# Attention scores as split products, with x parked in DRAM

## The chip, the cores and the metric

The kernel runs on one core of one Trainium2 chip, in one launch. The time is the device time of the whole program in microseconds (us), the median of a few executions. Engines are called TensorE (PE), VectorE (DVE), ScalarE (ACT), GpSimd (POOL) and SyncE (SP).

## The reference, cut to what matters

Two decoder layers on a sequence of 256 tokens with 2048 features, all in float32. Layer 0 has a convolution and DeltaNet mixer, layer 1 sparse attention; behind each mixer and behind each SwiGLU block stands a residual and a layer norm. The change lies in layer 1:

```
q, k_c, v_c, k_s, v_s, k_w, v_w, gates = split(x @ w_in)      # 16 query heads, 4 groups, head dim 128
q, k_s, k_w = rope(q), rope(k_s), rope(k_w)
k_cmp, v_cmp = compress(k_c), compress(v_c)                   # 15 compressed blocks per group
sc = einsum('bghsd,bgnd->bghsn', q, k_cmp) * 128 ** -0.5      # compressed branch
sc = einsum('bghqd,...', q, k_s or k_w)    * 128 ** -0.5      # selected and window branch
p = softmax(where(valid, sc, -1e30))                          # each branch
o = gate0 * p_c @ v_cmp + gate1 * p_s @ v_s + gate2 * p_w @ v_w
x = layer_norm(alpha * x + o @ w_out)
```

With 256 tokens all 4 blocks of 64 are selected and the window of 512 covers everything, so both the selected and the window branch are plain causal attention over 256 keys, each with keys and values of its own.

## The kernel before

Every dense product is done in three passes of split operands: a float32 array `w` is kept as `w_hi` (rounded to the fp32r format by a ScalarE copy, L708) and `w_lo` (the rest, a VectorE subtraction, L1253). `passes` (L2041) then issues hi x hi, hi x lo and lo x hi. Weights come in slabs of 1 MB, on SP's queue, into 4 `raw` slots, and are split by halves of a slab into 4 slots of `w_hi` and `w_lo`. `halves(n)` on ScalarE and on VectorE stands for the next n halves; ScalarE's waits until TensorE has used the half four before (`half_used`), VectorE's for ScalarE's, and TensorE's for VectorE's (`w_lo_ready`). The order of all work on each engine is written out by hand.

In layer 1 the four groups `g` of 4 query heads are worked through one after the other, with two tiles `t` of 128 tokens. For each, TensorE does:

- `scores(g, t)`: one PSUM bank `("c", g, t)` for the 4 heads against 15 compressed keys (L2595), and for each branch `b` `t + 1` banks `("s", g, t, b, k)` against `kn` = 128 (t + 1) keys (L2604). These are float32 matmuls of `qT` with `kcmpT` and `ksT`; each of them stands in the trace as two loads and two multiplies.
- `compressed_T`, `branch_T`: the scaled probabilities are turned.
- `outputs(g, t)`: the split probabilities times the split values, into `("ao", g, t)`.
- `queries(g + 1)`: the next group's turned queries, after VectorE's `rope`.
- `fill(n)`: n halves (12 passes each, two token tiles) of the query projection's next chunk, and behind its last, of the output projection `out1` (`out_halves`). For that product the attention output must be split too: `early_split(kt)` on both engines.

These use PSUM banks 4 to 7 in turn: use number `K[name]` must wait until use `K[name] - 4` has been read (`sp_free`).

VectorE in `scores(g, t)` (L1897) drains each bank with scale and mask (L1904, L1914) and takes the maximum of each branch (L1906, L1918), each of which releases ScalarE's `exps` of that branch (L1136). `scaled` multiplies by gate over sum (L1938, L1941). `put_T` (L1868) copies turned keys and queries out of PSUM (L1872). `compressed_lo`, `branch_lo` (L1956, L1964) and ScalarE's `compressed_hi`, `branch_hi` (L1149, L1157) split the turned probabilities. `rope_stage` (L1100) on ScalarE takes a chunk out of its banks for VectorE's `rope` (L1854 to L1866), `heads_out` (L1159) takes `ao` to `qT`.

The residual `x` stays in SBUF from the last norm on until `first_moments(2)` (L1374) adds it.

Of the kernel before, what the change touches and what calls it, by code (L numbers as in the profile page):

```python
# [13 lines left out]
F32 = mybir.dt.float32  # L14
# [7 lines left out]
P = 128  # L22
# [59 lines left out]
def trunk(nc, x_in, positions, ln_mix_g, ln_mix_b, ln_ffn_g, ln_ffn_b, ffn_w_in, ffn_w_out,  # L82
          hy_w_in, sc_conv_w, dn_conv_w, dn_a_log, dn_dt_bias, dn_norm_w, hy_w_out,
          nsa_w_in, cmp_pos_k, cmp_w1_k, cmp_w2_k, cmp_pos_v, cmp_w1_v, cmp_w2_v, nsa_w_out,
          inv_freq, ln_by_feature, end_positions, x_by_feature, gc_rows, beta_rows, out, stop=None):
# [3 lines left out]
    with ctx:  # L89
# [121 lines left out]
        kcmpT = part(64)  # L211
        assert used == 10944
# [20 lines left out]
        sc_buf = [[base[:, 1024 * n:1024 * n + 1024] for n in range(2)] for base in (gb_flat, sc_more)]  # L233
# [5 lines left out]
        v_cmp = sb("v_cmp", [P, NG * DH], F32R, offset=big_at + 4 * 10944)  # L239
        p_far = sb("p_far", [P, 2, 2, 512], F32R, offset=gb_at + 4 * 2048)  # L240
        p_near = [sb(f"p_near{n}", [P, 512], F32R, offset=gb_at + 4 * (512 + 1024 * n)) for n in range(2)]
# [5 lines left out]
        v_hi_ready, v_lo_ready = sem("v_hi_ready"), sem("v_lo_ready")  # L247

# [93 lines left out]
        def scores_use(g, t):  # L342
            uses([("c", g, t)] + [("s", g, t, b, k) for b in range(2) for k in range(t + 1)])
# [226 lines left out]
        def _(pool):  # L570
# [116 lines left out]
        def _(act):  # L687
# [401 lines left out]

            def put_hT(name):  # L1090
# [27 lines left out]
            halves(5)  # L1118
            name = ("vcmp",)
# [5 lines left out]
            halves(8)  # L1125
            keep_values(1, C["kv"] + 1)

            def exps(g, t, parts):
# [3 lines left out]
                for n in parts:  # L1132
                    act.wait_ge(for_act, FA[("scores", g, t, n)])
                    v = sc_buf[t][n - 1][:, 0:HPG * kn].rearrange("p (h n) -> p h n", h=HPG) if n else sc_cmp[t]
# [33 lines left out]
            values_hi(0)  # L1168
            exps(0, 0, range(3))
            halves(1)  # L1170
            for g in range(NG):
                exps(g, 1, (0, 1))
                halves(1)
                compressed_hi(g, 0)
# [23 lines left out]
                if g < NG - 1:  # L1198
                    exps(g + 1, 0, range(3))
# [15 lines left out]
        def _(dv):  # L1215
# [158 lines left out]
            def first_moments(n):  # L1374
# [3 lines left out]
                else:  # L1378
                    dv.wait_ge(x_in_sem, 16 * NT)
                for c in range(4):  # L1380
# [487 lines left out]
            def put_T(k, dst):  # L1868

                for a in range(2):  # L1870
                    dv.wait_ge(sp_ready[(k + a) % 4], (k + a) // 4 + 1)
                    dv.tensor_copy(dst(a), bank[4 + (k + a) % 4][:, :].rearrange("p (h t) -> p h t", h=2)).then_inc(sp_free[(k + a) % 4], 1)  # L1872
            for b in range(2):
# [6 lines left out]
                if b == 0:  # L1880
                    name = ("kcmpT",)
                    wait_sp(dv, name)
                    sp_out(dv.tensor_copy(kcmpT[:, 0:NCG], sp_bank(name)[:, 0:NCG]), name)
                else:
                    put_T(K[("kv", 0, 0)], lambda a: ksT[:, 0, 2 * a:2 * a + 2, :])
                rope(C["kv"] if b else C["kvk"])
            halves(8)
            put_T(K[("kv", 1, 0)], lambda a: ksT[:, 1, 2 * a:2 * a + 2, :])
# [8 lines left out]
            def scores(g, t):  # L1897
# [5 lines left out]
                v = sp_bank(name)[:, 0:HPG * NCMP].rearrange("p (h n) -> p h n", h=HPG)  # L1903
                sp_out(dv.scalar_tensor_tensor(sc_cmp[t], v, SCALE, bc(neg_cmp[:, t, :], HPG), ALU.mult, ALU.add), name)  # L1904
                wait_sp_read(dv, name)
                to_act(dv.tensor_reduce(nmax[:, 0:4], sc_cmp[t], AX.X, ALU.max, negate=True))  # L1906
                for b in range(2):
                    v = sc_buf[t][b][:, 0:HPG * kn].rearrange("p (h n) -> p h n", h=HPG)
                    hp = HPG // (t + 1)
# [821 lines left out]
```

## Time and profile before

| | us |
|---|---|
| median of 3 runs | 2351.47 (2351.12 to 2352.3) |
| the profiled execution | 2353.08, its span 2351.4 |
| TensorE multiply, loads | 2324.8, 1962.4 busy |
| VectorE, ScalarE, GpSimd | 1575.1, 1132.9, 34.3 busy |
| granted TensorE clock, mean | 0.998 |

All times in the trace are in us from the start of the span. A multiply's end is modelled, since matmuls are pipelined: what one costs is the distance to the next one's start. A row's bracket says how long the engine was idle ahead of it, and what released it.

### The profile page before, as it was taken

The page shows a single profiled execution, that of the slowest core. Times are in us where ns is not written, and L with a number is a line of the kernel's source. Part 1 is how long each engine was busy: PE and PEld are TensorE (multiplying, and loading weights), DVE is VectorE, ACT ScalarE, POOL GpSimd, SP SyncE. Part 2 cuts the span into 40 slices and gives each one's busy share as a digit, 9 for nine tenths or more (in the row PEclk, how much of TensorE's full clock was granted, in tenths as well). Part 3 has the DMA queues.
Part 4 walks back from the last instruction along what each step waited for, and adds up shares of the span by engine and source line. Part 5 has one row for each costly group of instructions (what it writes and reads, how often), then busy time and mean ns, then how long its engine had stood idle before and what let it go on. Part 6 is the DMA issues. An engine that isn't in the chain of part 4 may idle for free.

```text
span 2351.4 us, 30551 instructions
## 1 busy us (share of the span) xinstructions
PE 2324.8 (99%) x11559; PEld 1962.4 (83%) x11559; DVE 1575.1 (67%) x2075; ACT 1132.9 (48%) x1560; POOL 34.3 (1%) x79
## 2 busy tenths in 40 slices
PE   9999999999999999999999999999999999999998
PEld 8899988888888888888888887778888888888886
DVE  6767785676666666755578758867766666665556
ACT  5446654554434444444465546656444344444443
POOL 1000000100000000000000000000000000000001
PEclk9999999999999999999999999999999999999999
DMA  7555442745555555655546653254655565565553
GB/s 271 188 188 194 163 146 91 298 138 196 193 196 196 191 188 195 231 197 193 188 173 226 226 179 97 101 197 163 206 190 193 196 196 183 196 228 197 196 193 111
DMA packets 180486, 440.03 MB, mean 187 GB/s; under 512 B 7352, under 2 KB 19776, under 8 KB 166064
## 3 DMA queue, kind: packets, MB, share of 16 engines
q1 hardware_dynamic: 177456, 424.70, 53.8%
q0 software_dynamic: 2368, 13.13, 1.5%
q8 instruction: 54, 0.88, 0.2%
q10 hardware_dynamic: 576, 1.05, 0.1%
q14 instruction: 32, 0.26, 0.0%
HBM read 436.74 MB, written 2.11 MB: 187 GB/s over the span
## 4 chain that ended last, share of the span: by engine, by line
PE 88%; DVE 7%; ACT 4%; issue 1%; DMA 1%; SPq 0%; DVEq 0%; ACTq 0%
PE bank L2043 26%; PE bank L2045 26%; PE bank L2044 26%; PE bank L2056 4%; PE bank L2057 2%; DVE w_lo L1253 2%; PE bank L2381 1%; ACT w_hi L708 1%; DMA raw<-in_hy_w_in_dram 1%; ACT yt L783 1%; ACT sc_more L1136 1%; ACT gb L1136 1%; PE bank L2353 0%; DVE sm L1918 0%; ACT xt_both L794 0%
## 5 line engine op out<-in xcount | busy, mean ns | idle before, releaser
L1253 DVE TENSOR_TENSOR w_lo<-raw,w_hi 128x1024 fp32r<-128x1024 f32 x765 | 929.5, 1224 | 664.3 <-ACT w_hi L708 660.8
L708 ACT ACTIVATE w_hi<-raw 128x1024 fp32r<-128x1024 f32 x765 | 805.8, 1060 | 1007.8 <-PE bank L2045 922.2
L2043 PE MATMUL bank<-w_hi,xt_both 128*128 128x512 f32 x1888 | 740.9, 392 | 6.1 <-DVE w_lo L1253 2.8
L2045 PE MATMUL bank<-w_hi,xt_both 128*128 128x512 f32 x1888 | 735.9, 390 | 0.0
L2044 PE MATMUL bank<-w_lo,xt_both 128*128 128x512 f32 x1888 | 735.7, 390 | 0.0
L2043 PEld LDWEIGHTS bank<-w_hi,xt_both 128*128 128x128 f32 x1888 | 354.9, 188 | 80.8 <-issue 6.3
L2045 PEld LDWEIGHTS bank<-w_hi,xt_both 128*128 128x128 f32 x1888 | 354.8, 188 | 74.3
L2044 PEld LDWEIGHTS bank<-w_lo,xt_both 128*128 128x128 f32 x1888 | 354.9, 188 | 72.2
L2045 PE MATMUL bank<-w_hi,a_lo 128*128 128x512 f32 x664 | 258.4, 389 | 0.0
L2043 PE MATMUL bank<-w_hi,a_hi 128*128 128x512 f32 x664 | 258.4, 389 | 0.0
L2044 PE MATMUL bank<-w_lo,a_hi 128*128 128x512 f32 x664 | 258.4, 389 | 0.0
L2056 PE MATMUL bank<-xt_both,w_hi 128*128 128x512 f32 x488 | 172.8, 399 | 1.9 <-DVE xt_both L1510 1.3
L1468 DVE STREAM_TRANSPOSE big<-yt 32x256 f32<-32x256 f32 x352 | 153.5, 436 | 10.0
L2043 PEld LDWEIGHTS bank<-w_hi,a_hi 128*128 128x128 f32 x664 | 124.6, 188 | 26.1
L2045 PEld LDWEIGHTS bank<-w_hi,a_lo 128*128 128x128 f32 x664 | 124.6, 188 | 25.9
L2044 PEld LDWEIGHTS bank<-w_lo,a_hi 128*128 128x128 f32 x664 | 124.6, 188 | 25.7
L2057 PE MATMUL bank<-xt_both,w_lo 128*128 128x256 f32 x488 | 137.2, 281 | 0.0
L2043 PE MATMUL bank<-xt_both,w_hi 128*128 128x256 f32 x400 | 116.8, 292 | 0.3 <-DVE w_lo L1253 0.3
L2045 PE MATMUL bank<-xt_both,w_lo 128*128 128x256 f32 x400 | 113.2, 283 | 0.0
L2044 PE MATMUL bank<-xt_both,w_hi 128*128 128x256 f32 x400 | 113.2, 283 | 0.0
L2056 PEld LDWEIGHTS bank<-xt_both,w_hi 128*128 128x128 f32 x488 | 91.8, 188 | 25.2 <-DVE xt_both L1510 1.6
L2057 PEld LDWEIGHTS bank<-xt_both,w_lo 128*128 128x128 f32 x488 | 92.2, 189 | 0.0
(343 smaller groups left out, 1794.0 us busy)
## 6 DMA issues: line engine op xcount, KB each, us to landing
raw<-in_ffn_w_in_dram SPq DMA_DIRECT2D x176, 1024.0 KB, 5.0
raw<-in_ffn_w_out_dram SPq DMA_DIRECT2D x88, 1024.0 KB, 4.9
raw<-in_hy_w_in_dram SPq DMA_DIRECT2D x53, 1024.0 KB, 5.1
raw<-in_nsa_w_in_dram SPq DMA_DIRECT2D x41, 1024.0 KB, 5.1
raw<-in_hy_w_out_dram SPq DMA_DIRECT2D x16, 1024.0 KB, 5.0
raw<-in_nsa_w_out_dram SPq DMA_DIRECT2D x16, 1024.0 KB, 5.1
raw<-in_cmp_w_k_dram SPq DMA_DIRECT2D x4, 1024.0 KB, 6.8
raw<-in_cmp_w_v_dram SPq DMA_DIRECT2D x4, 1024.0 KB, 6.4
```

Source lines behind the costliest of these rows:

```text
L708: act.activation(weights_of(h)[0], half_of(h), ACT.Copy).then_inc(w_hi_ready, 1)
L783: ins = act.activation(yt[:, kt, tok], src[:, a * P:(a + 1) * P], ACT.Identity, bias=lnT[:, 1, kt:kt + 1], scale=lnT[:, 0, kt:kt + 1])
L1136: ins = act.activation(v[:, h, :], v[:, h, :], ACT.Exp, bias=nmax[:, 4 * n + h:4 * n + h + 1], accum_out=sums[:, 4 * n + h:4 * n + h + 1])
L1253: dv.tensor_tensor(lo, src, hi.bitcast(F32), ALU.subtract).then_inc(w_lo_ready, 1)
L1468: ins = dv.transpose(dst, src)
L2043: pe.matmul(dst, l_hi, r_hi, start=start, stop=False, skip_group_check=shared)
L2044: pe.matmul(dst, l_hi, r_lo, start=False, stop=False, skip_group_check=shared)
L2045: return pe.matmul(dst, l_lo, r_hi, start=False, stop=stop, skip_group_check=shared)
L2056: pe.matmul(b[f][:, :], hi[:, v], xt_both[:, kt, :, :], start=kt == 0, stop=False, skip_group_check=True)
L2057: ins = pe.matmul(b[f][:, 0:SEQ], lo[:, v], xt_hi[:, kt, :], start=False, stop=kt == KT - 1, skip_group_check=True)
L2381: ins = pe.matmul(b[:, h * P:(h + 1) * P], lhs(h), rhs(h), start=True, stop=True)
```

## The change

- The turned keys go, split, to `k_split`, in place of `x`: `[hi/lo, group, branch, token]`, so that the two branches' keys of a group lie side by side. The turned queries of one group go to `q_split`. ScalarE copies the high part out of PSUM (`keys_hi`, `queries_hi`), VectorE subtracts (`turned_lo_out`, in place of `put_T`). The compressed keys are split by VectorE alone, with 16 columns a group.
- `scores` issues three passes for each head: 16 columns for the compressed keys, `2 * kn` for both branches at once. A bank `("s", g, t, k)` now holds both branches of 2 heads (t = 0) or of 1 head (t = 1). VectorE drains all banks of a tile, and then takes the two maxima.
- `x` is stored to DRAM on POOL's queue after the loads of `w2`, and loaded again after `("ao", 3, 0)`; ScalarE waits for the store ahead of `keys_hi(0)`, VectorE for the load in `first_moments(2)`.
- In TensorE's loop `fill(1), outputs(g, 0), fill(1)` becomes `fill(2), outputs(g, 0)`. On ScalarE `rope_stage` comes before `heads_out` and `compressed_hi`, and in group 3 the early splits before `compressed_hi(3, 0)`. In group 2 the splits 2 and 3 come before VectorE's `rope` and ScalarE's `branch_hi(2, 1)`.
- The buffers of scores and probabilities are laid out anew (`sc_both`, `probs`, `p_near`).

```
@@ POOL, ahead of layer_norm(2)
+                for t in range(NT):
+                    pool.dma_start(x_rows[t * P:(t + 1) * P, :], x[:, t, :]).then_inc(x_out, 16)
+                pool.wait_ge(x_out, 16 * NT)
+                wait_sp(pool, ("ao", NG - 1, 0))
+                for t in range(NT):
+                    pool.dma_start(x[:, t, :], x_rows[t * P:(t + 1) * P, :]).then_inc(x_back, 16)
@@ ScalarE
+            def queries_hi(g):
+                for a in range(2):
+                    name = ("q", 2 * g + a)
+                    wait_sp(act, name)
+                    act.activation(q_split[:, 0, 2 * a:2 * a + 2, :], sp_bank(name)[:, :].rearrange("p (h t) -> p h t", h=2), ACT.Copy)\
+                       .then_inc(t_hi_ready, 1)
...
             halves(5)
+            act.wait_ge(x_out, 16 * NT)
+            keys_hi(0)
             name = ("vcmp",)
             wait_sp(act, name)
...
             for g in range(NG):
                 exps(g, 1, (0, 1))
                 halves(1)
+                if g == NG - 1:
+                    for kt in range(8, EARLY["out1"]):
+                        early_split("out1", kt)
                 compressed_hi(g, 0)
                 for b in range(2):
                     branch_hi(g, 0, b)
                 exps(g, 1, (2,))
                 halves(3)
-                heads_out(g, 0)
-                if g == NG - 1:
-                    for kt in range(8, EARLY["out1"]):
-                        early_split("out1", kt)
                 if g == NG - 2:
                     for kt in range(2):
                         early_split("out1", kt)
-                compressed_hi(g, 1)
                 if g < NG - 1:
                     rope_stage(C["q"] + g + 1, FA[("rope", g)])
-                for b in range(2):
-                    branch_hi(g, 1, b)
+                heads_out(g, 0)
+                compressed_hi(g, 1)
                 if g == NG - 2:
                     for kt in range(2, 4):
                         early_split("out1", kt)
+                for b in range(2):
+                    branch_hi(g, 1, b)
...
                 halves(2)
                 if g < NG - 1:
+                    queries_hi(g + 1)
                     exps(g + 1, 0, range(3))
@@ VectorE
-            def put_T(k, dst):
+            def turned_lo_out(name, n, hi, lo):
+                dv.wait_ge(t_hi_ready, n)
+                dv.tensor_tensor(lo, sp_bank(name)[:, :].rearrange("p (h t) -> p h t", h=2), hi.bitcast(F32), ALU.subtract)\
+                  .then_inc(sp_free[K[name] % 4], 1)
...
-                    sp_out(dv.tensor_copy(kcmpT[:, 0:NCG], sp_bank(name)[:, 0:NCG]), name)
+                    own(dv.tensor_scalar(kcmp_split[:, :, :].rearrange("p a n -> p (a n)"), ones[:, :], 0.0, None, ALU.mult))
...
+                    own(dv.tensor_copy(hi, src))
+                    sp_out(dv.tensor_tensor(lo, src, hi.bitcast(F32), ALU.subtract), name)
... in scores(g, t)
+                for k in range(2 * (t + 1)):
+                    name = ("s", g, t, k)
+                    wait_sp(dv, name)
+                    ins = dv.scalar_tensor_tensor(both[:, 2 * hp * k:2 * hp * (k + 1), :], sp_bank(name)[:, :].rearrange("p (m n) -> p m n", n=kn),
+                                                  SCALE, bc(mask, 2 * hp), ALU.mult, ALU.add)
+                    sp_out(ins, name)
+                for k in range(2 * (t + 1)):
+                    wait_sp_read(dv, ("s", g, t, k))
                 for b in range(2):
+                    v = probs(t, b)
                     to_act(dv.tensor_reduce(nmax[:, 4 + 4 * b:8 + 4 * b], v, AX.X, ALU.max, negate=True))
@@ TensorE
                 for h in range(HPG):
-                    ins = pe.matmul(b[:, h * NCMP:(h + 1) * NCMP], qT[:, 4 * g + h, v], kcmpT[:, g * NCMP:(g + 1) * NCMP], start=True, stop=True)
+                    ins = passes(b[:, 16 * h:16 * h + 16], q_split[:, 0, h, v], q_split[:, 1, h, v], *kc, True, True)
...
+                for k in range(2 * (t + 1)):
+                    name = ("s", g, t, k)
+                    b = sp_use(name)
+                    for j in range(hp):
+                        h = hp * k + j
+                        ins = passes(b[:, j * 2 * kn:(j + 1) * 2 * kn], q_split[:, 0, h, v], q_split[:, 1, h, v], *keys, True, True)
+                    sp_done(ins, name)
...
-                fill(1)
+                fill(2)
                 outputs(g, 0)
-                fill(1)
                 compressed_T(g, 1)
```

## Rows read from the trace of the kernel before

**Rows 1.** The page's busy times of the engines, shares of the span.
```profile
PE 2324.8 (99%) x11559; PEld 1962.4 (83%) x11559; DVE 1575.1 (67%) x2075; ACT 1132.9 (48%) x1560; POOL 34.3 (1%) x79
```

**Rows 2.** Waits, 1395 to 1560 us: who for whom, total, times, longest.
```profile
PEld bank L2625 <- DVE p_cmp L1956: 2.5, 4, 0.9
PE bank L2043 <- ACT yt L1104: 1.7, 1, 1.7
...
PE bank L2043 <- DVE p_far L1964: 1.3, 4, 0.3
PE bank L2043 <- DVE xt_both L1291: 1.2, 1, 1.2
```

**Rows 3.** Timeline of TensorE, score blocks: start, length, line, shapes, count.
```profile
1440.32 0.96 PE L2595 MATMUL bank<-big 128*128 128x15 f32 x8
1441.13 2.03 PE L2604 MATMUL bank<-big 128*128 128x128 f32 x16
1442.92 0.48 PE L2043 MATMUL bank<-w_hi,xt_both 128*128 128x512 f32 x1
...
1530.54 3.70 PE L2604 MATMUL bank<-big 128*128 128x256 f32 x16
1533.89 0.58 PE L2043 MATMUL bank<-w_hi,xt_both 128*128 128x512 f32 x1
```

**Rows 4.** Timeline of TensorE, split products of 512 and 256 columns.
```profile
1229.04 0.39 PE L2056 MATMUL bank<-xt_both,w_hi 128*128 128x512 f32 x1
1229.26 0.28 PE L2057 MATMUL bank<-xt_both,w_lo 128*128 128x256 f32 x1
1229.38 0.40 PE L2056 MATMUL bank<-xt_both,w_hi 128*128 128x512 f32 x1
```

**Rows 5.** Timeline of group 0, second tile, 1412 to 1428 us.
```profile
1412.72 1.28 DVE L1914 SCALAR_TENSOR_TENSOR sc_more<-bank,big 128x512 f32<-128x512 f32 x2
...
1415.35 0.51 ACT L1136 ACTIVATE sc_more<-sc_more,sm 128x256 f32<-128x256 f32 x1 [1.25 <-DVE sm L1918]
...
1418.42 1.23 DVE L1253 TENSOR_TENSOR w_lo<-raw,w_hi 128x1024 fp32r<-128x1024 f32 x1 [0.58 <-ACT w_hi L708]
...
1425.49 3.49 DVE L1253 TENSOR_TENSOR w_lo<-raw,w_hi 128x1024 fp32r<-128x1024 f32 x3
...
1427.24 0.48 PE L2043 MATMUL bank<-w_hi,xt_both 128*128 128x512 f32 x1
```

**Rows 6.** Timeline of group 1, first tile, 1442 to 1448 us.
```profile
1442.31 0.69 DVE L1914 SCALAR_TENSOR_TENSOR gb<-bank,big 128x512 f32<-128x512 f32 x1 [0.52 <-PE bank L2604]
...
1443.75 0.40 ACT L1136 ACTIVATE gb<-gb,sm 128x128 f32<-128x128 f32 x1 [0.66 <-DVE sm L1918]
...
1447.05 0.23 DVE L1929 RECIPROCAL sm<-sm 128x12 f32<-128x12 f32 x1 [1.88 <-ACT gb L1136]
```

**Rows 7.** Timeline of group 3, 1545 to 1550 us.
```profile
1545.88 1.33 ACT L727 ACTIVATE xt_both<-big 128x256 fp32r<-128x256 f32 x4
...
1546.32 1.43 DVE L1291 TENSOR_TENSOR xt_both<-big,xt_both 128x256 fp32r<-128x256 f32 x4 [0.60 <-ACT xt_both L727]
...
1549.04 0.47 PE L2043 MATMUL bank<-w_hi,xt_both 128*128 128x512 f32 x1 [1.42 <-DVE w_lo L1253]
```

**Rows 8.** Timeline of the turned keys, 1344 to 1352 us.
```profile
1344.61 1.17 ACT L1122 ACTIVATE v_cmp<-bank 15x512 fp32r<-15x512 f32 x2
...
1346.00 0.68 DVE L1878 TENSOR_TENSOR v_cmp<-bank,v_cmp 15x512 fp32r<-15x512 f32 x1
1346.71 1.29 DVE L1872 COPY big<-bank 128x512 f32<-128x512 f32 x2
...
1351.85 0.85 PEld L2570 LDWEIGHTS bank<-ident,yt 128*128 128x128 f32 x8 [0.57 <-DVE yt L1866]
```

**Rows 9.** DMA issues (KB each, us to landing) and POOL's timeline.
```profile
x<-in_x_dram POOLq DMA_DIRECT2D x2, 1024.0 KB, 10.0
...
1242.12 0.72 POOL L661 DMA_DIRECT2D big<-in_cmp_w_k_dram  x1 [274.80 <-DVE x L1414]
```

More of the change, by code:

```diff
@@ L210, in trunk @@
         cmp_hT = part(128, "p (k n) -> p k n", k=2)
-        kcmpT = part(64)
-        assert used == 10944
+        kcmp_at = big_at + 4 * used
+        used += 128
+        assert used == 11008
         used += NG * DH
@@ L232, in trunk, with probs @@
         sc_more = sb("sc_more", [P, 2048], offset=a_at)
-        sc_buf = [[base[:, 1024 * n:1024 * n + 1024] for n in range(2)] for base in (gb_flat, sc_more)]
+        sc_both = [gb_flat[:, 0:1024], sc_more[:, 0:2048]]
+        def probs(t, b):
+            return sc_both[t].rearrange("p (h b n) -> p h b n", h=HPG, b=2)[:, :, b, :]
         kc_flat = kcT.rearrange("p b h t -> p (b h t)")
@@ L247, in trunk @@
         v_hi_ready, v_lo_ready = sem("v_hi_ready"), sem("v_lo_ready")
+        t_hi_ready, x_out, x_back = sem("t_hi_ready"), sem("x_out"), sem("x_back")
         def unit_no(g, t, b, k=0):
@@ L342, in scores_use @@
         def scores_use(g, t):
-            uses([("c", g, t)] + [("s", g, t, b, k) for b in range(2) for k in range(t + 1)])
+            uses([("c", g, t)] + [("s", g, t, k) for k in range(2 * (t + 1))])
         def probs_use(g, t):
@@ L1088, in _, with keys_hi @@
                .then_inc(sp_free[K[("gates",)] % 4], 1)
+            def keys_hi(b):
+                for a in range(2):
+                    name = ("kv", b, a)
+                    wait_sp(act, name)
+                    act.activation(k_split[:, 0, 2 * a:2 * a + 2, b, :], sp_bank(name)[:, :].rearrange("p (h t) -> p h t", h=2), ACT.Copy)\
+                       .then_inc(t_hi_ready, 1)
+            def queries_hi(g):
+                for a in range(2):
+                    name = ("q", 2 * g + a)
+                    wait_sp(act, name)
+                    act.activation(q_split[:, 0, 2 * a:2 * a + 2, :], sp_bank(name)[:, :].rearrange("p (h t) -> p h t", h=2), ACT.Copy)\
+                       .then_inc(t_hi_ready, 1)
             def put_hT(name):
@@ L1125, in _ @@
             halves(8)
+            keys_hi(1)
             keep_values(1, C["kv"] + 1)
@@ L1168, in _ @@
             values_hi(0)
+            queries_hi(0)
             exps(0, 0, range(3))
@@ L1379, in first_moments @@
                     dv.wait_ge(x_in_sem, 16 * NT)
+                if n == 2:
+                    dv.wait_ge(x_back, 16 * NT)
                 for c in range(4):
@@ L1969, in turned_q @@
             def turned_q(g):
-                put_T(K[("q", 2 * g)], lambda a: qT[:, 4 * g + 2 * a:4 * g + 2 * a + 2, :])
+                for a in range(2):
+                    hi, lo = (q_split[:, n, 2 * a:2 * a + 2, :] for n in range(2))
+                    turned_lo_out(("q", 2 * g + a), 4 + 2 * g + a + 1, hi, lo)
             halves(3)
@@ L1993, in _ @@
                 compressed_lo(g, 1)
+                if g == NG - 2:
+                    for kt in range(2, 4):
+                        early_split("out1", kt)
                 if g < NG - 1:
@@ L2593, in scores @@
                 b = sp_use(name)
+                kc = [kcmp_split[:, n, 16 * g:16 * g + 16] for n in range(2)]
                 for h in range(HPG):
-                    ins = pe.matmul(b[:, h * NCMP:(h + 1) * NCMP], qT[:, 4 * g + h, v], kcmpT[:, g * NCMP:(g + 1) * NCMP], start=True, stop=True)
+                    ins = passes(b[:, 16 * h:16 * h + 16], q_split[:, 0, h, v], q_split[:, 1, h, v], *kc, True, True)
                 sp_done(ins, name)
                 kn = (t + 1) * P
-                hp = HPG // (t + 1)
-                for br in range(2):
-                    for k in range(t + 1):
-                        name = ("s", g, t, br, k)
-                        b = sp_use(name)
-                        for h in range(hp):
-                            ins = pe.matmul(b[:, h * kn:(h + 1) * kn], qT[:, 4 * g + hp * k + h, v], ksT[:, br, g, 0:kn], start=True, stop=True)
-                        sp_done(ins, name)
+                hp = 2 // (t + 1)
+                keys = [k_split[:, n, g, :, 0:kn] for n in range(2)]
+                for k in range(2 * (t + 1)):
[5 more added lines that the diff above has]
+                    sp_done(ins, name)
             def compressed_T(g, t):
```

45 lines of the change are left out of this document (21 added, 24 removed).

## The prediction, before the change was run

> **What bounds the kernel now.** I read the page's busy table first, then the waits of the attention stage, then the three engines' instructions in order of time. The table says that TensorE works through the whole span [rows 1]: a change pays only if it takes TensorE work away, or takes away one of the few places where TensorE waits. The waits [rows 2] name those places, about 9 us in all where the four heads' groups are worked through (1402 to 1562 us): in each group's `outputs(g, 0)`, which waits for VectorE's low parts (the 2.5 and 1.3 us), in group 2 for ScalarE's `rope_stage` and for an early split, and in group 3 for a low half of weights [rows 7]. Everywhere else there a fill (a half slab of the next dense product, 12 passes) follows without a gap. Behind the attention stage TensorE again works without gaps, so what is late or early at its end is late or early at the end of the span, one for one.
>
> **The score products themselves.** Today one compressed block of scores takes 1440.32 to 1441.13 = 0.81 us, a `t == 0` block 1441.13 to 1442.92 = 1.79 us, a `t == 1` block 1530.54 to 1533.89 = 3.35 us [rows 3]. A float32 matmul stands in the trace as two load-and-multiply records (4 heads give x8), 0.10 to 0.11 us each when it has few columns. The split form has 3 records of 4 heads = 12 in each block: 512 columns cost 0.22 to 0.23 us a record, 256 columns 0.12 [rows 3, 4]. So `t == 1` falls to 12 x 0.227 = 2.72 (-0.63), `t == 0` to 12 x 0.12 = 1.44 (-0.35). For 16 moving columns the trace has no split product. Nearest are the float32 records with 15 columns: 12 x 0.112 = 1.35 (+0.5). If the load of 128 stationary columns were hidden, it could be as little as 0.3 in all; the upper bound is a doubled record, 2.7. I take 1.35, since 15 and 128 columns cost nearly the same today (0.10 and 0.11) [rows 3], so it is the load that is paid. Per group: -0.63 - 0.35 + 2 x 0.5 = 0.0. The products save TensorE nothing.
>
> The Trainium skill (TensorE: Matmul & The Clock Gate, "Back-to-back issue gap") puts a matmul of 1 to 64 columns at a floor of about 25 ns, and its section "LDWEIGHTS (loading the stationary operand)" a load at columns / 1.2, 107 ns for 128. By the first alone the compressed block would cost 0.3 us; by the second 1.28. The rows side with the second.
>
> **The order of VectorE and ScalarE.** This is where I expect the time to go. A bank now holds both branches of the same heads. Before, VectorE drained branch 0 (2 steps), reduced it to its maximum, and ScalarE began its exponentials while VectorE did branch 1. Now all four banks are drained before the first maximum. In group 0, `t == 1`: two drains from 1412.72 take 1.28, ScalarE's exponentials start 1415.35, its next weight half lies behind them, and VectorE's low half waits 0.58 for that, until 1418.42 [rows 5]. Two more drains lie before the first maximum: +1.22 (two of 0.62, less one wait). ScalarE has no gap from 1415.35 on that could take this up: exponentials, half, `compressed_hi`, `branch_hi`, exponentials of branch 1, and then VectorE's scaling and its next low halves, the first done at about 1426.7 [rows 5] (three from 1425.49 in 3.49). TensorE needs that half at 1427.24: slack 0.55.
>
> For `t == 0` the same: a first drain at 1442.31, exponentials from 1443.75, and VectorE sits idle 1.88 until they end [rows 6]; now compressed block +0.5 and one more drain before the maximum, less 0.2 for the shorter bank: about +0.87 on the exponentials, hence on the next halves and on the start of `scores(g, 1)`. It adds to the first. So the first half behind `scaled(g, 1)` comes 0.87 + 1.22 = 2.1 us later, minus the slack 0.55: **+1.5 us in group 0 and +1.5 in group 1**, although the fill put ahead of `outputs(g, 0)` (one fill, 12 x 0.227 = 2.7 us, against (2.5 + 1.3) / 4 = 0.95 us of waits there) does hide the low parts; the wait moves to the halves behind it.
>
> Group 2. The waits for `rope_stage` (1.7) and for the early split (1.2) [rows 2]. The first is bounded anew: ScalarE now stages rope before `heads_out` and `compressed_hi`, but its exponentials end 2.1 us later, and by my count it ends where it did: 0. The second goes, since VectorE splits 2 and 3 before rope: -1.4 with its restart. **-1.4 in group 2.** What is late next there is VectorE, which reaches `scores(3, 0)` some 0.5 us behind TensorE: +0.4 into group 3.
>
> Group 3. ScalarE's four early splits (1.33 us from 1545.88, VectorE's wait of 0.60 on them, VectorE's half behind them, TensorE's wait 1.42 [rows 7]) now stand ahead of `compressed_hi`. They delay ScalarE's chain by 1.3 and save the 0.6: 0.87 + 1.22 + 0.4 + 1.3 - 0.6 = 3.2 on a half that is already late, less 0.1. **+3.1.**
>
> **Keys and queries.** The copies out of PSUM become a ScalarE copy and a VectorE subtraction. VectorE pays the same (two copies 1.29, one subtraction 0.68 [rows 8]). ScalarE pays about 1 us for each pair (two copies of 512 columns take 1.17). `queries_hi` is free: TensorE runs 2.7 us of fill or 3 us of outputs before the scores that need it. `keys_hi(0)` is not: it stands ahead of `vcmp` on ScalarE (1344.61), for which VectorE waits (1346.00), behind which come keys and rope, and TensorE waits already 0.57 for that rope at 1351.85 [rows 8]: **+0.8**. `keys_hi(1)` lies in idle time. VectorE's three instructions for `kcmpT` (+0.7 us in place of one copy) fall where the low halves lead by more than that: 0, at most +0.7.
>
> **x to DRAM and back.** Two stores behind the `w2` loads at 1242.12 and two loads behind `ao(3, 0)`, at about 1544. Two loads of this size landed in 10.0 us beside the weights [rows 9]. The store has until the first `keys_hi` at 1344, the load until `first_moments(2)`, behind over ten more fills of 2.7 us: both hidden, taken as 0. If the stores, which meet weight loads, made one slab late, +1 to +5. The wait `x_back` on VectorE has nothing to wait for; were it late, the whole norm would queue behind it. POOL's queue takes the new waits ahead of the loads of the norm's gains, which aren't issued before 1561 anyway.
>
> **Sum.** 1.5 + 1.5 - 1.4 + 3.1 + 0.8 = +5.5; for overlaps that I counted as strict I take 0.3 off: +5.2 us. On the profiled span of 2351.4: 2356.6, with the 1.7 us around it 2358.3 for that execution. It ran 1.6 above the median of 2351.47, so as a median 2356.7; I say **2356.5**.
>
> **Rivals.**
> A. The reorder does what its places suggest: the waits at `outputs(g, 0)` (3.8 us), and the early split's 1.4 vanish and ScalarE's chain has more room than I count, because VectorE's and TensorE's waits on each other soak it up. For it: VectorE has idle stretches of 0.5 to 1.9 us per group [rows 6]. Against: they lie behind the exponentials and not ahead of them. -5 us: 2346.5.
> B. Small products are paid by columns: compressed block 0.3 us in place of 1.35. Then the `t == 0` maximum isn't late (0.87 falls to -0.2): 1.07 less in each of four groups, +5.2 - 4.2 = +1.0: 2352.5. The same time comes out if half of the ScalarE delay is soaked up. The skill's 25 ns floor, named above, is this rival's rule.
> C. The stores of x collide with the weight loads, or the loads back with `w_out`'s, and ScalarE waits for a slab: +5 on top, 2361.5. It decides once a slab lands more than some 5 us late. Slower side, with my own forecast.
> D. The split has no effect on TensorE's records (each stays two-fold): `t == 1` 24 records, 5.4 us: +2 x 4 and more, 2370.
>
> **Chances.** Forecast 0.42, A 0.24, B 0.25, C 0.07, D 0.02. The range runs from A's time to C's edge: 2346 to 2361. A measurement of this kernel tells 0.2%, 4.7 us, from no change. Faster than 2346.8: most of A, 0.22. Slower than 2356.2: half of the forecast's mass and more (0.29), C, D and a tail of B: 0.40. Same: 0.38.
>
> **What would show it.** After: the compressed block's records x96, some 0.11 apart; the branches' x48 of 256 and x48 of 512 columns, 0.12 and 0.23 apart; no wait of TensorE for `p_far` or `p_cmp`; a new wait of TensorE for L1253's `w_lo` in each group, behind the transposes of `t == 1`, of 1 to 1.5 us, and before `outputs` of about 0.7; ScalarE's exponentials of branch 0 beginning 2.6 + 1.2 us behind VectorE's first drain; a wait of about 1.4 us for rope at the kv transposes. I am wrong if TensorE takes the halves behind `scaled(g, 1)` without waiting, or if the 16-column records stand closer than 0.06.

## The result and the profile after

| kernel | median us (lowest to highest) | ratio to before, 95% interval |
|---|---|---|
| before | 2351.16 (2350.3 to 2352.68) | |
| after | 2358.93 (2356.7 to 2360.41) | 1.0036 [1.0026, 1.0045] |

The change costs 7.8 us. The profiled execution of the kernel after took 2360.28 us, its span 2358.6, against 2351.4 before. The page of after, busy times, and the costliest form of multiply (busy, mean ns | idle before it, and what ended it), beside [rows 1]:

```profile
PE 2326.7 (99%) x11559; PEld 1961.9 (83%) x11559; DVE 1575.3 (67%) x2077; ACT 1139.1 (48%) x1572; POOL 36.4 (2%) x83
...
L2096 PE MATMUL bank<-w_hi,xt_both 128*128 128x512 f32 x1888 | 740.2, 392 | 10.6 <-DVE w_lo L1289 8.7
```

TensorE has the same number of records and 1.9 us more of busy time, of which about 1.1 us are a longer stretch at a lower clock (last section): the products cost nearly as much as before. The rest is waiting. The waits of after, 1395 to 1575 us, beside [rows 2]:

```profile
PE bank L2096 <- DVE w_lo L1289: 7.3, 7, 2.6
...
PEld bank L2096 <- DVE big L1953: 4.5, 4, 2.3
...
PE bank L2096 <- DVE big L1953: 2.8, 4, 1.9
...
PE bank L2096 <- DVE xt_both L1327: 1.7, 1, 1.7
```

The waits for `p_cmp` and `p_far` are gone. Waits for low halves of weights, seven of them, stand in their place. The wait for `L1953` has grown: the fifth bank of a `t == 1` tile takes the place of the compressed bank, which VectorE must have drained. The kernel before had the same wait in group 0 alone, for its drain L1904 (waits of before, 1395 to 1560 us):

```profile
PE bank L2604 <- DVE big L1904: 0.9, 1, 0.9
```

Now it stands in every group: 1.87 us in group 0, 0.30 in each of the others.

TensorE's timeline in group 3, its two score blocks, beside [rows 3]:

```profile
1524.45 0.37 PE L2096 MATMUL bank<-k_split,q_split 128*128 128x256 f32 x1
...
1525.96 0.40 PE L2096 MATMUL bank<-w_hi,xt_both 128*128 128x512 f32 x1
...
1531.43 0.25 PE L2096 MATMUL bank<-kcmp_split,q_split 128*128 128x16 f32 x1
1531.54 0.26 PE L2097 MATMUL bank<-kcmp_split,q_split 128*128 128x16 f32 x1
...
1532.77 0.48 PE L2096 MATMUL bank<-k_split,q_split 128*128 128x512 f32 x1
...
1535.40 0.50 PE L2096 MATMUL bank<-k_split,q_split 128*128 128x512 f32 x1 [0.30 <-DVE big L1953]
...
1536.20 0.40 PE L2096 MATMUL bank<-w_hi,xt_both 128*128 128x512 f32 x1
```

A compressed block takes 1532.77 - 1531.43 = 1.34 us (1.25 for `t == 0`, 1523.20 to 1524.45; before 0.81), its records 0.11 apart; `t == 0` takes 1.51 (before 1.79); `t == 1` takes 3.43 with its wait (before 3.35), and 2.84 to 2.86 in groups 1 to 3 of the kernel by_heads below, which does not wait there. Without the wait a group's products cost TensorE 0.45 + 0.53 - 0.28 - 0.49 = 0.2 us more than before.

Group 0, second tile, all engines' timeline, beside [rows 5]:

```profile
1412.76 2.47 DVE L1962 SCALAR_TENSOR_TENSOR sc_more<-bank,big 128x512 f32<-128x512 f32 x4
...
1415.37 2.35 DVE L1969 TENSOR_REDUCE sm<-sc_more 128x4 f32<-128x1024 f32 x2
...
1416.62 0.51 ACT L1170 ACTIVATE sc_more<-sc_more,sm 128x256 f32<-128x256 f32 x1 [2.47 <-DVE sm L1969]
...
1419.68 1.23 DVE L1289 TENSOR_TENSOR w_lo<-raw,w_hi 128x1024 fp32r<-128x1024 f32 x1 [1.97 <-ACT w_hi L723]
...
1420.96 0.50 PE L2096 MATMUL bank<-w_hi,xt_both 128*128 128x512 f32 x1 [0.53 <-DVE w_lo L1289]
...
1428.14 0.47 PE L2096 MATMUL bank<-w_hi,xt_both 128*128 128x512 f32 x1 [1.20 <-DVE w_lo L1289]
```

All four drains stand ahead of the first maximum; ScalarE is idle 2.47 us where it was idle 1.25, VectorE waits 1.97 us for ScalarE's half where it waited 0.58, and TensorE pays twice, 0.53 and 1.20.

Group 1, first tile, VectorE's and ScalarE's timelines, beside [rows 6]:

```profile
1443.48 1.41 DVE L1962 SCALAR_TENSOR_TENSOR gb<-bank,big 128x512 f32<-128x512 f32 x2 [0.35 <-PE bank L2098]
1445.00 1.28 DVE L1969 TENSOR_REDUCE sm<-gb 128x4 f32<-128x512 f32 x2
...
1445.72 0.40 ACT L1170 ACTIVATE gb<-gb,sm 128x128 f32<-128x128 f32 x1 [1.28 <-DVE sm L1969]
...
1449.01 0.23 DVE L1980 RECIPROCAL sm<-sm 128x12 f32<-128x12 f32 x1 [2.60 <-ACT gb L1170]
```

Counted from the block's start at 1441.22, the exponentials begin 4.50 us later; before it was 1443.75 - 1440.32 = 3.43.

A group's period, from its first compressed record to the next group's (group 3: to the end of `outputs(3, 1)`), worked out from the traces:

| us | group 0 | 1 | 2 | 3 |
|---|---|---|---|---|
| before | 37.65 | 38.88 | 42.39 | 39.62 |
| after | 39.57 | 40.76 | 41.21 | 45.10 |
| difference | +1.92 | +1.88 | -1.18 | +5.48 |

The granted clock of TensorE fell to half inside group 3 of the trace of after, and that is worth 2.7 of the 5.48 us (last section).

### The profile page after: what moved, and what is told of

Same layout as the page of the kernel before. It is cut to its first block, busy times and chain, and to the rows that moved or that the text cites. A ratio compares the mean times of both kernels' runs of the same rounds, so it can differ in the third digit from the quotient of the medians.

```text
span 2358.6 us, 30575 instructions
## 1 busy us (share of the span) xinstructions
PE 2326.7 (99%) x11559; PEld 1961.9 (83%) x11559; DVE 1575.3 (67%) x2077; ACT 1139.1 (48%) x1572; POOL 36.4 (2%) x83
## 4 chain that ended last, share of the span: by engine, by line
PE 88%; DVE 6%; ACT 4%; issue 1%; DMA 1%; SPq 0%; DVEq 0%; ACTq 0%
PE bank L2096 26%; PE bank L2098 26%; PE bank L2097 26%; PE bank L2109 4%; PE bank L2110 2%; DVE w_lo L1289 2%; PE bank L2434 1%; ACT w_hi L723 1%; ACT sc_more L1170 1%; ACT yt L798 1%; DMA raw<-in_hy_w_in_dram 1%; ACT gb L1170 1%; DVE sc_more L1962 0%; DVE sc_more L1992 0%; PE bank L2406 0%
```

## The experiments

Each is timed in five rounds against the kernel before, whose median in these comparisons was 2350.41 to 2350.81; in the result's own comparison it was 2351.16. A gain on the kernel after, given below as a difference of medians, is therefore some 0.4 to 0.8 us too large. There were 11 executions of each kernel, but 5 of order_of_before, 6 of keys_early and 7 of splits_back. A step of about 1 us is near the noise, so it is read from the traces as well. Medians:

| kernel | us | ratio, 95% interval |
|---|---|---|
| park_only | 2350.86 | 1.0 [0.9991, 1.0009] |
| reorder_only | 2348.98 | 0.999 [0.9981, 0.9999] |
| order_of_before | 2362.35 | 1.0049 [1.0036, 1.0063] |
| by_branch | 2354.37 | 1.0016 [1.0007, 1.0025] |
| keys_early | 2358.07 | 1.0032 [1.002, 1.0044] |
| splits_back | 2357.79 | 1.0029 [1.0018, 1.004] |
| one_pass | 2355.94 | 1.0021 [1.0012, 1.003] |
| after_spread | 2354.83 | 1.0018 [1.0008, 1.0027] |
| combined | 2349.56 | 0.9996 [0.9987, 1.0005] |
| by_heads | 2346.63 | 0.9983 [0.9974, 0.9992] |
| reorder_splits | 2347.36 | 0.9986 [0.9977, 0.9995] |
| reorder_spread | 2345.35 | 0.9978 [0.9969, 0.9987] |

**park_only.** The kernel before, with nothing but the parking of `x`: the two stores, the two loads, and the wait for each.

```
+  x -> x_rows behind the loads of w2; x_rows -> x behind ("ao", 3, 0)
+                if n == 2:
+                    dv.wait_ge(x_back, 16 * NT)
```

> The kernel before with x stored to DRAM behind the w2 loads and loaded again after ao(3, 0), nothing else. Theory: hidden, 2351.2 within 0.7. Rival (the stores and loads make slabs late): 2354 or more.

It costs nothing. In the kernel after, POOL's timeline and the DMA issues (KB each, us to landing) say why:

```profile
1241.72 1.09 POOL L672 DMA_DIRECT2D x_rows_dram<-x  x2
1548.94 1.06 POOL L676 DMA_DIRECT2D x<-x_rows_dram  x2 [306.12 <-PE bank L2098]
```

```profile
x_rows_dram<-x POOLq DMA_DIRECT2D x2, 1024.0 KB, 10.3
x<-x_rows_dram POOLq DMA_DIRECT2D x2, 1024.0 KB, 6.0
```

The store has landed some 90 us before the first `keys_hi`, the load by about 1555.

**reorder_only.** The kernel before with nothing but the new order of the engines' work.

```
-                fill(1)
+                fill(2)
                 outputs(g, 0)
-                fill(1)
                 compressed_T(g, 1)
... ScalarE and VectorE: rope and the early splits placed as in the change
```

> The kernel before with only the new order of fills, rope_stage, heads_out and early splits; float32 scores, banks by branch, x stays in SBUF. Theory (the maxima of the side-by-side banks come late and push the halves behind scaled): without that push the order gives what its places suggest: no wait at outputs(g, 0) (3.8 us), rope_stage and the early split of group 2 (2.5 us), some of it taken back by the halves that are next: 2346 to 2347.5. Rival (the new order itself makes the halves late): 2355 or more.

-1.8 us: 2348.98, where I expected 2346 to 2347.5. Its periods are 37.29, 38.47, 38.95, 41.67: groups 0 to 2 gain 0.36, 0.41, 3.44, and group 3 loses 2.05. TensorE's timeline and the windows of the same stretch (us, busy times of PE, PEld, DVE, ACT, POOL, granted clock, DMA share, GB/s) show on what:

```profile
1543.48 0.77 PE L2043 MATMUL bank<-w_hi,xt_both 128*128 128x512 f32 x1 [2.61 <-DVE w_lo L1253]
```

```profile
1543.00:1547.00 4.00, 3.52 (x9) 2.83 (x10) 3.94 (x6) 0.30 (x1) 0.00 (x0) 0.57 0.36 80
```

The fill and the eight turned blocks behind that wait take 5.08 us, against 3.64 in the kernel before: 1.4 of the 2.05 us are the lower clock, and 0.6 are left for the longer wait.

**order_of_before.** The other half: the kernel after with the old order, as the diff above read backwards.

> The kernel after with the old order of fills and of ScalarE and VectorE. Theory: the push of about 2 us on the first half behind scaled stays in every group, and the group 2 waits come back: 2.5 us above the kernel after, 2361. Rival (the order is at fault): near 2352.

Without the new order the change costs 11.5 us in place of 7.8. TensorE's timeline there, ahead of `outputs(1, 0)` and `outputs(2, 0)`:

```profile
1461.28 0.50 PE L2680 MATMUL bank<-p_cmp,v_cmp 79*128 79x512 f32 x1 [1.88 <-DVE p_cmp L2007]
...
1504.04 0.49 PE L2680 MATMUL bank<-p_cmp,v_cmp 79*128 79x512 f32 x1 [1.87 <-DVE p_cmp L2007]
```

The lateness is still there. TensorE meets it here at the outputs (1.88 us in group 1), and in the kernel after, in the same group, with 0.52 ahead of the outputs and 1.24 behind the transposes. The waits of group 2 for `rope_stage` (1.74) and for the early split (1.24) are back as well, as expected.

**by_branch.** The kernel after, but at `t == 1` a bank holds one branch of two heads again (24 passes of 256 columns in place of 12 of 512), drained and reduced branch by branch.

```
+                if t:
+                    for k in range(4):            # branch k // 2, heads 2 * (k % 2) and the next
+                        ... passes(b[:, j * kn:(j + 1) * kn], q_split[..h, v], k_split[:, n, g, k // 2, 0:kn])
... VectorE: two drains, maximum of branch 0, two drains, maximum of branch 1
```

> The kernel after, but for t = 1 each bank holds one branch of two heads (24 passes of 256 columns in place of 12 of 512, +0.16 us), so that VectorE again takes the first maximum after two drains. Theory: 1.2 us less push in each of four groups: 2354 to 2355. Rival (late splits of the query, x to DRAM, or the passes' own time): no less than 2358.

-4.6 us, though TensorE has 24 x 0.12 - 12 x 0.227 = 0.16 us more of work in a group. TensorE's wait ahead of `outputs(g, 0)` is gone, and the one behind the transposes is smaller (TensorE's timeline in group 1; in the kernel after 1.24):

```profile
1464.79 0.47 PE L2108 MATMUL bank<-w_hi,xt_both 128*128 128x512 f32 x1 [0.83 <-DVE w_lo L1289]
```

Groups 0 to 2 are 0.71, 1.19 and 1.19 us shorter than in the kernel after (38.86, 39.57, 40.02), where I had counted 1.22 a group for the two drains.

**keys_early.** The kernel after, with `keys_hi(0)` one half slab earlier on ScalarE.

```
-            halves(5)
+            halves(4)
             act.wait_ge(x_out, 16 * NT)
             keys_hi(0)
+            halves(1)
```

> The changed kernel, but keys_hi(0) stands one half slab earlier on ScalarE, ahead of the last of the five halves in front of vcmp. If keys_hi(0) just ahead of vcmp is what made the turned keys late (my step +0.8; the traces show +0.73), VectorE reaches v_cmp and the rope behind it 0.7 us earlier: TensorE's wait for rope at the transposes of kv falls from 1.3 to about 0.6 us, and the time is about 2358.1. Rival: the copies only change places with a half that is then late by as much (1.17 us on ScalarE): 2358.9 or a little above, with a new wait of TensorE for w_lo at about 1340 us.

-0.9 us, as expected, with no new wait. With 6 executions that is not clear of noise (the difference of the medians has a 95% interval of -2.4 to +1.2 us); the trace decides. The kernel after's timeline, of ScalarE, VectorE and TensorE, has the chain, beside [rows 8]:

```profile
1342.82 1.07 ACT L1110 ACTIVATE k_split<-bank 128x512 fp32r<-128x512 f32 x2
1343.78 1.17 ACT L1155 ACTIVATE v_cmp<-bank 15x512 fp32r<-15x512 f32 x2
...
1344.98 0.68 DVE L1923 TENSOR_TENSOR v_cmp<-bank,v_cmp 15x512 fp32r<-15x512 f32 x1 [0.80 <-ACT v_cmp L1155]
...
1350.83 0.42 PEld L2623 LDWEIGHTS bank<-ident,yt 128*128 128x128 f32 x4 [1.33 <-DVE yt L1904]
```

In keys_early the last of these waits is (waits of that kernel, 1330 to 1395 us):

```profile
PEld bank L2624 <- DVE yt L1905: 0.6, 1, 0.6
```

That is the 0.57 us of the kernel before. The multiply's own wait there, 0.92 us in the kernel after, is gone.

**splits_back, reorder_splits.** The kernel after, and reorder_only, with the four early splits of group 3 behind `heads_out(3, 0)` again on ScalarE.

```
                 halves(1)
-                if g == NG - 1:
-                    for kt in range(8, EARLY["out1"]):
-                        early_split("out1", kt)
                 compressed_hi(g, 0)
...
                 heads_out(g, 0)
+                if g == NG - 1:
+                    for kt in range(8, EARLY["out1"]):
+                        early_split("out1", kt)
```

> The changed kernel, but in group 3 ScalarE's four early splits (8 to 11 of out1, 1.33 us) stand again behind heads_out(3, 0), as before the change. If they are what lengthens group 3's chain (my step: +1.3 - 0.6), group 3's period falls from 45.1 us by 0.7 to 1.0, TensorE's wait for w_lo behind the transposes of t == 1 falls from 2.8 to about 1.5 to 2.1 us, and the time is about 2357.5 to 2358.2; if the stretch of lower granted clock that follows that wait goes with it, another 1.5 to 2.5 us less, about 2356. Rival: the chain of group 3 is set by the late maximum alone and the four splits lie in slack: 2358.9, and TensorE's wait for p_far's low part or the splits comes back at outputs(3, 0).

> The kernel before with the new order of outputs and engines (as reorder_only), but the four early splits of group 3 stay behind heads_out(3, 0). reorder_only measured 2349.0, and its trace shows TensorE waiting 2.8 us for w_lo in group 3 and then 3.4 us at the lower clock. If the early splits make that wait, it is down to about 1.5 to 2.1 us: 2348.1, and 2346.5 if the stretch at the lower clock goes as well. Rival: they lie in slack, 2349.0.

-1.1 and -1.6 us, the second with an interval of -2.7 to 0.0. In the traces the waiting shrinks by less. In splits_back TensorE's wait behind the transposes did not fall to between 1.5 and 2.1 us, as I had expected, but rose from 2.61 to 3.21, while the 0.23 and 0.53 us of waiting at the transposes went. Group 3's period falls from 45.10 to 43.46, and 1.1 of these 1.6 us are the clock, which was low for 3.4 us in place of 6.8. In reorder_splits the period falls from 41.67 to 41.31.

And in reorder_splits TensorE's wait is hardly shorter than reorder_only's 2.61 (timeline of TensorE, group 3), since the splits stand on VectorE ahead of the same halves, with 0.60 us of waiting for ScalarE:

```profile
1542.60 0.61 PE L2043 MATMUL bank<-w_hi,xt_both 128*128 128x512 f32 x1 [2.48 <-DVE w_lo L1253]
```

So my account of that wait (1.3 us on ScalarE) was incomplete, which led to reorder_spread and after_spread below.

**one_pass.** The kernel after, with the compressed branch's scores in one pass; it leaves out the two products with a low part.

```
-                    ins = passes(b[:, 16 * h:16 * h + 16], q_split[:, 0, h, v], q_split[:, 1, h, v], *kc, True, True)
+                    ins = pe.matmul(b[:, 16 * h:16 * h + 16], q_split[:, 0, h, v], kc[0], start=True, stop=True)
```

> The changed kernel, but the compressed branch's scores are made with one pass of three (the two products with a low part are left out of these scores), so a compressed block of TensorE has 4 records in place of 12, 0.42 us in place of 1.26. If the compressed block of t == 0 sets how late VectorE and ScalarE are in every group (my step: +0.5 each, 0.87 with the extra drain), each group's period falls by 0.8 us for t == 0 and by up to 0.8 for t == 1: -3.3 to -6.5 us, 2352.5 to 2355.5. Rival: half of it is soaked up, because VectorE waits for the second bank of scores all the same: -1.7 us, about 2357. Other rival, TensorE's own work alone counts where it has no wait: the compressed blocks cost it 8 x 0.84 = 6.7 us, all of it saved: 2352.2.

-3.0 us. Groups 0 to 2 are each 0.9 us shorter (38.66, 39.89, 40.33), and two blocks a group became 0.9 us cheaper each (0.36 and 0.44 us): one block's worth arrives, and the other doesn't. Where the `t == 1` block's goes is one wait of TensorE, in group 1 of one_pass and of after:

```profile
1450.78 0.50 PE L2096 MATMUL bank<-k_split,q_split 128*128 128x512 f32 x1 [1.23 <-DVE big L1953]
```

```profile
1453.44 0.50 PE L2096 MATMUL bank<-k_split,q_split 128*128 128x512 f32 x1 [0.30 <-DVE big L1953]
```

It grows by 0.93: VectorE's drain of the compressed bank, not TensorE, sets when the fifth bank can begin.

**reorder_spread, after_spread.** The four early splits of group 3 leave the chain on both engines, on top of reorder_splits and of splits_back (where ScalarE had them behind `heads_out(3, 0)`).

```
... ScalarE
             for g in range(NG):
+                if g == NG - 1:
+                    for kt in range(8, EARLY["out1"]):
+                        early_split("out1", kt)
                 exps(g, 1, (0, 1))
... VectorE
                 scores(g, 1)
+                if g == NG - 1:
+                    early_split("out1", 8)
                 halves(1)
... and behind scaled(g, 1)
-                if g == NG - 1:
-                    for kt in range(8, EARLY["out1"]):
-                        early_split("out1", kt)
                 halves(1)
+                if g == NG - 1:
+                    for kt in range(9, EARLY["out1"]):
+                        early_split("out1", kt)
```

> The kernel before with the new order of outputs and engines, and in group 3 the four early splits taken out of the chain: ScalarE does them ahead of exps(3, 1), where it sits idle 1.86 us, VectorE does number 8 behind scores(3, 1), where it waits 0.58 us for ScalarE's half, and 9 to 11 one half later. If VectorE's 0.60 of waiting and 1.43 us of splits ahead of its halves are what TensorE's 2.5 us wait for w_lo in group 3 is made of, that wait falls to about 0.5 us: from 2347.4 to 2345.4, and 2343.7 if the stretch at the lower clock behind it goes too. Rival: number 9 or 10 is then late for the fill that reads it, or the products wait for p_far instead: 2347.4 or more.

> The changed kernel with the same placing of the four early splits of group 3. My reading of the changed kernel is that 2.7 us of group 3's loss are these splits on ScalarE (1.33) and VectorE (0.60 + 1.43) ahead of late halves; splits_back gave back 1.1. Now group 3's period falls from 43.5 us (splits_back) to about 41.5: 2355.8, and 2354 without a stretch at the lower clock behind it. Rival: ScalarE's chain from the late maximum sets group 3, the splits on VectorE were slack: 2357.8.

-3.0 us on splits_back (2357.79 to 2354.83) and -2.0 on reorder_splits. TensorE's wait in reorder_spread, same place as the rows of reorder_splits and reorder_only above, and the windows of that stretch, with the granted clock at 1.00:

```profile
1538.99 0.47 PE L2045 MATMUL bank<-w_hi,xt_both 128*128 128x512 f32 x1 [0.43 <-DVE w_lo L1253]
```

```profile
1543.00:1547.00 4.00, 4.00 (x20) 3.39 (x21) 4.00 (x6) 3.23 (x5) 0.00 (x0) 1.00 0.57 231
```

The two gains are not waiting alone. Group 3 is 2.98 us shorter than in reorder_splits (38.33) and 2.93 shorter than in splits_back (40.53), and 1.6 us of each are a stretch at the lower clock that is gone, which leaves 1.3 to 1.4 us for the splits.

The kernel that keeps the old products and takes the new order with these splits has the lowest median of all, 0.9978 [0.9969, 0.9987].

**combined.** by_branch, keys_early and after_spread at once.

> The changed kernel with all parts of my explanation taken back that can be without giving up its split products: t == 1 banks of one branch (by_branch gave -4.6 us), keys_hi(0) one half earlier (-0.85), the four early splits of group 3 out of the chain (-1.1 to -3). If these are separate causes they add up: 2358.9 - 4.6 - 0.85 - 2 = 2351.5 (2350.5 to 2352.5). What would be left against reorder_spread is the 0.9 us a group of t == 0, the compressed blocks' 0.45 us each where nothing soaks them up, some 5 us. Rival: the causes overlap (each took away the same wait in group 3): 2353 to 2354.

2349.56, better than I expected: the sum of the three alone, -4.56 - 0.86 - 4.10 = -9.52, is what the three give together, -9.37. Each set against the kernel before of its own comparison, that is -8.1 and -8.7. They add up, so they are separate causes.

**by_heads.** As combined, but the banks of both branches stay; VectorE and ScalarE go by pairs of heads.

```
-                for k in range(2 * (t + 1)):
-                    ... drain bank k
-                for b in range(2):
-                    v = probs(t, b)
-                    to_act(dv.tensor_reduce(nmax[:, 4 + 4 * b:8 + 4 * b], v, AX.X, ALU.max, negate=True))
+                for j in range(2):
+                    for k in range(j * (t + 1), (j + 1) * (t + 1)):
+                        ... drain bank k
+                    pair_max = nmax[:, 4:12].rearrange("p (b h) -> p h b", b=2)[:, 2 * j:2 * j + 2, :]
+                    to_act(dv.tensor_reduce(pair_max, ... both branches of heads 2 * j, 2 * j + 1))
... ScalarE's exps part n: both branches of heads 2 * n - 2, 2 * n - 1
```

> The changed kernel with its cheap products of both branches side by side kept, but VectorE takes the maxima and ScalarE the exponentials by pairs of heads (both branches of heads 0 and 1, then of 2 and 3) and not by branches, so that the first maximum again follows half of the drains; with keys_hi(0) one half earlier and the four early splits of group 3 placed as in after_spread. If what the side-by-side banks cost is only that the first maximum waits for all drains, t == 0 gains as t == 1 does: against combined (2349.6, t == 1 banks of one branch, 24 passes) 0.6 to 0.9 us a group for t == 0 and 0.16 a group for the 12 passes, 2346.0 to 2347.0. Rival: the compressed blocks at 1.26 us instead of 0.81 are what is left of the loss, and the drains of t == 0 lie in slack: 2349. From the side of TensorE's own work (t == 0 -0.27, t == 1 -0.63 a group) it could come to 2344 if the late halves were soaked up.

2346.63, inside what was expected, and 12.3 us below the kernel after. Group 0, second tile, VectorE's, ScalarE's and TensorE's timelines, to be read against the ones of after above:

```profile
1411.11 1.28 DVE L1964 SCALAR_TENSOR_TENSOR sc_more<-bank,big 128x512 f32<-128x512 f32 x2
1412.49 1.22 DVE L1970 TENSOR_REDUCE sm<-sc_more 128x4 f32<-128x1024 f32 x1
...
1413.75 0.51 ACT L1171 ACTIVATE sc_more<-sc_more,sm 128x256 f32<-128x256 f32 x1 [1.25 <-DVE sm L1970]
...
1416.81 1.23 DVE L1290 TENSOR_TENSOR w_lo<-raw,w_hi 128x1024 fp32r<-128x1024 f32 x1 [0.58 <-ACT w_hi L723]
...
1425.26 0.47 PE L2099 MATMUL bank<-w_hi,xt_both 128*128 128x512 f32 x1 [0.86 <-DVE w_lo L1290]
```

ScalarE's 1.25 and VectorE's 0.58 are those of the kernel before [rows 5], with the new products. Periods: 37.55, 38.74, 39.20, 38.64, in each group 0.68 to 0.83 us less than in combined (38.31, 39.57, 39.98, 39.32). In groups 0 and 1, which the earlier keys and the spread splits leave as long as in the kernel after (39.58 and 40.79, 39.55 and 40.79), the whole loss of 1.9 us is gone: the kernel before has 37.65 and 38.88.

## Why the prediction was right, and where a size was off

It said 2356.5 (2346 to 2361), slower or the same; measured 2358.93. The signs it named for TensorE are there: no wait for `p_far` or `p_cmp`, waits of 0.52 to 0.65 us ahead of the outputs, and of 1.20 to 2.61 behind the transposes. Its steps:

- **Products save TensorE nothing.** Right: 12 records of 0.11 us for the compressed block (1.25 to 1.34 against 1.35), 1.51 against 1.44, and 2.86 against 2.72. Rival B (16 columns paid by columns) is ruled out by the 0.11. one_pass, where the block costs 0.36, shows what it would have been worth: 3.0 us of the 4.2 I gave it.
- **First maximum behind all drains: +1.5 in groups 0 and 1.** Right in kind, measured +1.92 and +1.88. ScalarE's exponentials begin 1416.62 - 1412.76 = 3.86 us after the first drain (I said 3.8), and 1.07 us later than before in `t == 0` (I said 0.87). by_branch and by_heads show that this is the cause and not a companion. What I missed is that TensorE's wait at the fifth bank of `t == 1` would grow: 0.30 in place of none, and in group 0 1.87 in place of 0.88.
- **Group 2, -1.4.** Measured -1.18, but not by the route I gave: the early split's wait did not go, it moved behind the transposes (1.66 us). The `rope_stage` wait, which I had left at zero gain, is the one that went.
- **Group 3, +3.1.** This is the mis-sized term: +5.48. Of it 2.7 are a stretch at half the granted clock (below), for which the prediction had no term; that leaves +2.8. The early splits stand in the chain on both engines, and I had counted ScalarE's 1.3 and VectorE's wait of 0.6 only. after_spread takes them out and gives back 4.1 us by the medians. In the traces group 3 falls by 4.57 us, from 45.10 to 40.53: 1.9 of it is waiting, and 2.7 is the stretch at the lower clock, which is not in the trace of after_spread.
- **Keys, +0.8.** Right: the transposes came 0.77 us late, with 1.33 of wait in place of 0.57, and in keys_early that wait is 0.57 again.
- **Parking x, 0.** Right: 2350.86 against 2350.81. Rival C is out.
- **The new order.** Rival A gave it 5 us; it is worth 1.8 on the old products and 3.4 on the new. It hides the waits at `outputs(g, 0)` and gains 4.2 us in groups 0 to 2, but group 3 took 41.67 us with its early splits, 38.33 with them spread; order and spread splits together are worth 5.1 us. A's mechanism was there, and in group 3 one misplaced step and the stretch at the lower clock behind it took half of it back.

The steps add up: the four periods and the keys give 1.92 + 1.88 - 1.18 + 5.48 + 0.77 = 8.9 us. TensorE came to the turned keys 1.8 us earlier in the trace of after than in that of before, 1.6 of it because only the trace of before has a stretch at the lower clock at 370 us. With 0.1 us more behind the attention stage that makes 7.2, as the spans differ. Without the 2.7 us of clock in group 3 the steps come to 6.2 us, where the prediction had added up 5.5. So the mechanism and the main sizes were right; that the profiled execution, 2360.3 us, came so near the 2358.3 given for it was in part luck, since the two stretches at the lower clock, 2.7 us in one trace and 1.6 in the other, partly cancel. Which of the other executions had such stretches is not known.

What remains between by_heads and reorder_spread, 1.3 us, is not clear of noise by the medians (interval -3.1 to +0.6 us) and was not taken apart. In the traces by_heads is 0.25 to 0.31 us longer in each group. The compressed blocks' 0.45 us each may be the reason, which is argued and not shown.

## What to carry to other kernels

When two results are put into one buffer or bank, ask which of them the next engine waited for: the consumer's first step now waits for both. Restore the pipeline by cutting the work the way the banks are now cut (by heads), not the way it used to be (by branch); here banks of one branch gave back 4.56 us at `t == 1`, and going on from there to both-branch banks reduced by heads gave another 2349.56 - 2346.63 = 2.9, which is what `t == 0` is worth together with the 12 passes of `t == 1`. And ask of a low-cost step placed ahead of a late one (the early splits) on every engine that has it, not on one: the same four splits stood in the chain twice.

## What the runs showed of the hardware that was not expected

Apart from the last microseconds of the program, the granted clock of TensorE fell to half, for 3.4 us at a time and once for 6.8, one to three times in nine of the fourteen traces, at places where TensorE had waited or had just run short products. The windows of after (us, busy times of PE, PEld, DVE, ACT, POOL, then the granted clock, DMA share, GB/s), group 3:

```profile
1548.00:1552.00 4.00, 2.09 (x14) 1.16 (x12) 3.93 (x9) 3.99 (x6) 1.06 (x2) 1.00 0.44 153
1552.00:1556.00 4.00, 2.54 (x6) 2.08 (x7) 3.97 (x5) 1.25 (x3) 0.00 (x0) 0.56 1.00 394
1556.00:1560.00 4.00, 4.00 (x16) 3.22 (x16) 1.59 (x3) 0.37 (x1) 0.00 (x0) 0.59 0.67 247
```

And its timeline of TensorE at the start and the end of that stretch:

```profile
1553.46 0.76 PE L2096 MATMUL bank<-w_hi,xt_both 128*128 128x512 f32 x1 [2.61 <-DVE w_lo L1289]
...
1555.30 0.63 PE L2097 MATMUL bank<-w_lo,xt_both 128*128 128x512 f32 x1
1555.73 0.63 PE L2098 MATMUL bank<-w_hi,xt_both 128*128 128x512 f32 x1
...
1558.72 1.31 PE L2406 MATMUL bank<-ident,sc_more 128*128 128x128 f32 x8
1559.79 0.48 PE L2096 MATMUL bank<-w_hi,xt_both 128*128 128x512 f32 x1
```

Records stand 0.43 us apart in place of 0.23, so this is the 1.2 GHz level: from 1553.46 to 1559.79, 12 passes and 8 turned blocks take 6.33 us, against 3.64 in the kernel before and 3.62 in one_pass, 2.7 us more. The trace of before has such a stretch elsewhere, of which its windows show:

```profile
370.00:374.00 4.00, 4.00 (x16) 3.12 (x14) 3.02 (x5) 0.63 (x2) 0.00 (x0) 0.57 0.11 41
```

There TensorE came from 64-column products and one wait of 0.55 us. The kernel after runs the same 12 passes there at full clock, in 2.9 us in place of 4.5, so such a stretch in one profile is no property of the kernel. Nor does each long wait bring one: the 2.61 us wait of group 3 had one beside it in after, reorder_only, by_branch and keys_early, and not in one_pass, which has the same wait. What decides between them stays open.

Nor does each stretch cost time. In group 0 of splits_back and of keys_early 3.4 us at half the clock (from 1412.87 and from 1414.66 us) left the period as it was, 39.56 and 39.58 against 39.57 in the kernel after: TensorE's next two waits, 0.53 and 1.20 us there, shrank to a single one of 0.47 and 0.49. Slow products ahead of a wait only use up the wait. The four kernels with the splits spread, whose wait in group 3 is 0.43 to 1.19 us, have none in group 3 or elsewhere; 1.6 us of what reorder_spread gains on reorder_splits, and after_spread on splits_back, is that in the traces. Whether a shorter wait prevents the stretch, or these four executions happened to have none, is not shown.

One more difference between the traces lies ahead of the change. In seven of the fourteen TensorE is 1.5 to 2.8 us earlier at about 335 us from the start than in the other seven, though all these kernels do the same work up to there; the cause is not known. The spans of two profiles can therefore not be compared at 2 us; the periods of the groups can.
